# The first block of the input weights asked for by ScalarE's queue, beside x on SyncE's

## The reference, cut to what matters

```python
h = rms_norm(x, attn_norm_w[l])          # x (256, 1024)
proj = h @ w_in[l]                       # w_in (1024, 3072)
dq, dk, dv, lq, lk, lv = jnp.split(proj, split_at, axis=-1)
o_diff = rms_norm(diff_attention(dq, dk, dv, diff_slopes, lam), diff_subln_w[l]) * (1.0 - lam_init)
o_dil = dilated_attention(lq, lk, lv, dil_slopes)
mix = jnp.concatenate([o_diff.reshape(...), o_dil.reshape(...)], axis=-1)
x = x + mix @ w_out[l]
x = x + moe_ffn(rms_norm(x, ffn_norm_w[l]), ...)   # top 4 of 32 experts, 12 MB of weights each
return rms_norm(x, final_norm_w)
```

## Time and profile before

| | us |
|---|---|
| median of 3 runs | 1051.96 (1050.82 to 1052.12) |
| the profiled execution | 1052.54 |
| its span in the trace | 1050.8 |
| PE busy | 1010.7 (96%) |
| VectorE, ScalarE, GpSimd busy | 231.3, 118.1, 21.7 |
| moved by DMA | 423.85 MB, 403 GB/s over the span |

### The profile page before, as it was taken

How to read it: one execution, slowest core, us unless ns; L and a number is a source line. 1 busy time by engine, 2 the same in 40 slices (tenths; PEclk the granted TensorE clock), 3 DMA queues, 4 the chain that set the end, 5 groups by cost and what they waited for, 6 DMA issues and landing times.

```text
span 1050.8 us, 11954 instructions
## 1 busy us (share of the span) xinstructions
PE 1010.7 (96%) x4953; PEld 431.2 (41%) x4953; DVE 231.3 (22%) x515; ACT 118.1 (11%) x275; POOL 21.7 (2%) x39
## 2 busy tenths in 40 slices
PE   9999999999999999999999999898998989899996
PEld 8686543434343434343434333242433333243422
DVE  3766542221111111111111111021211111021111
ACT  1143411110100000000000000000000000000001
POOL 1001400000000000000000000000000000000000
PEclk9999999999999999999999999999999999999999
DMA  9991869999999999999999999999999999999996
GB/s 302 417 408 31 314 240 400 423 427 428 435 430 433 428 430 438 424 435 437 425 435 432 428 437 428 432 438 424 435 434 427 437 430 429 429 426 427 427 424 252
DMA packets 28458, 423.85 MB, mean 403 GB/s; under 512 B 5440, under 2 KB 5456, under 8 KB 11312
## 3 DMA queue, kind: packets, MB, share of 16 engines
q1 hardware_dynamic: 26112, 422.80, 95.3%
q10 hardware_dynamic: 2320, 0.67, 0.3%
HBM read 422.41 MB, written 1.05 MB: 403 GB/s over the span
## 4 chain that ended last, share of the span: by engine, by line
PE 72%; DMA 19%; DVE 5%; another core or an unknown queue 1%; SPq 1%; ACT 1%; issue 1%; DVEq 0%; POOL 0%
PE psum L996 35%; DMA gu_ring<-in_w_gate_up_dram 18%; PE psum L1047 11%; PE psum L1069 5%; PE psum L953 4%; PE psum L663 3%; PE psum L821 3%; PE psum L710 3%; PE psum L686 3%; DVE mixed L1494 2%; DVE mixed L1490 1%; DVE mixed L1492 1%; PE psum L706 1%; PE psum L692 1%
## 5 line engine op out<-in xcount | busy, mean ns | idle before, releaser
L996 PE MATMUL psum<-gu_ring,mixed 128*64 128x512 f32 x2048 | 455.3, 601 | 21.7 <-DMA gu_ring<-in_w_gate_up_dram 21.4
L996 PEld LDWEIGHTS psum<-gu_ring,mixed 128*64 128x64 f32 x2048 | 145.4, 138 | 310.4 <-issue 271.3
L1490 DVE TENSOR_SCALAR mixed<-psum 128x512 f32<-128x512 f32 x32 | 22.1, 691 | 411.3 <-PE psum L996 411.3
L1047 PE MATMUL psum<-dn_ring,mixed 128*64 128x512 f32 x352 | 78.0, 595 | 2.2 <-ACT mixed L595 2.2
L1047 PE MATMUL psum<-mixed 128*64 128x512 f32 x352 | 78.0, 595 | 0.0
L1447 DVE TENSOR_TENSOR mixed<-posm,iota 128x256 f32<-128x256 f32 x47 | 19.9, 424 | 243.4 <-PE psum L663 243.0
L613 ACT ACTIVATE mixed<-psum 128x512 f32<-128x512 f32 x30 | 17.9, 597 | 433.2 <-PE psum L996 433.2
L972 PE MATMUL psum<-mixed 64*128 64x512 f32 x256 | 63.6, 615 | 0.7 <-ACT mixed L599 0.7
L953 PE MATMUL psum<-mixed,xres 128*128 128x128 f32 x480 | 56.2, 275 | 0.0
L953 PEld LDWEIGHTS psum<-mixed,xres 128*128 128x128 f32 x480 | 55.2, 193 | 0.0
L663 PE MATMUL psum<-ident,mixed 128*128 128x128 f32 (+1 forms) x251 | 48.1, 300 | 4.2
(11 more groups left out here) (168 smaller groups left out, 537.1 us busy)
## 6 DMA issues: line engine op xcount, KB each, us to landing
gu_ring<-in_w_gate_up_dram SPq DMA_DIRECT2D x44, 4096.0 KB, 45.4
gu_ring<-in_w_gate_up_dram SPq DMA_DIRECT2D x34, 2048.0 KB, 18.7
dn_ring<-in_w_down_dram SPq DMA_DIRECT2D x11, 4096.0 KB, 43.6
mixed<-in_w_down_dram SPq DMA_DIRECT2D x11, 4096.0 KB, 44.8
dn_ring<-in_w_down_dram SPq DMA_DIRECT2D x9, 2048.0 KB, 19.1
mixed<-in_w_down_dram SPq DMA_DIRECT2D x7, 2048.0 KB, 16.5
gu_ring<-in_w_in_dram SPq DMA_DIRECT2D x11, 1024.0 KB, 16.6
gu_ring<-in_w_gate_up_dram SPq DMA_DIRECT2D x10, 1024.0 KB, 8.7
```

The source lines that it names most:

```text
L996: last = mm(bank[b0 + b][CAP * c:CAP * (c + 1), :], xg[:, k, CAP * half:CAP * (half + 1)], group(w, c), start=False, stop=(k == KT - 1), s ...
L1047: last = mm(bank[4][CAP * c:CAP * (c + 1), :], actT[:, a0:a0 + CAP], dn_whole[half][:, k // 2, w0:w0 + 512], start=False, stop=(k == KT - ...
L1490: chain(V.tensor_scalar(up_t, bank[b0 + 1][:, :], 1.0 - LIMIT, 1.0 + LIMIT, ALU.max, ALU.min))
```

## The change

The load of block k = 0 of the first weight group leaves SyncE's list, where it stood behind the two halves of x, and becomes the first instruction of ScalarE's list, ahead of the two norm rows. Source, destination, size and semaphore stay. On SyncE's list block k = 1 now follows x directly.

```diff
@@ block.sync
                 sp.dma_start(xres[:, a, :], xv[:, a, :]).then_inc(x_in[a], 16)
 
             w_in_v = w_in.rearrange("o (k p) c -> p (o k) c", p=P)
-            for k in range(2):
-                sp.dma_start(gu_ring[:, 0, D * k:D * (k + 1)], w_in_v[:, k, 0:D]).then_inc(w_in_first[k], 16)
+            sp.dma_start(gu_ring[:, 0, D:2 * D], w_in_v[:, 1, 0:D]).then_inc(w_in_first[1], 16)
             for g in range(3):
@@ block.scalar
         def _(act):
+            act.dma_start(gu_ring[:, 0, 0:D], w_in.rearrange("o (k p) c -> p (o k) c", p=P)[:, 0, 0:D])\
+                .then_inc(w_in_first[0], 16)
             act.dma_start(prm_rows[0:8, :], attn_norm_w.rearrange("o (k p) -> (o k) p", p=P)).then_inc(prm_in, 16)
             act.dma_start(prm_rows[8:16, :], ffn_norm_w.rearrange("o (k p) -> (o k) p", p=P)).then_inc(prm_in, 16)
```

## The result

| | before | after |
|---|---|---|
| median of 11 runs, us | 1051.3 (1050.56 to 1053.41) | 1054.74 (1053.3 to 1055.51) |
| ratio | | 1.0030, 95% interval 1.0022 to 1.0037 |
| the profiled execution | 1052.54 | 1053.59 |
| its span | 1050.8 | 1051.9 |

The change makes the kernel slower by 3.4 us, 0.3%. The forecast was 1052.9 and "the same"; the range (1050.7 to 1054.8) holds the median, at its upper edge. The eleven times of after say why to be careful with that: five lie between 1053.3 and 1054.1, six between 1054.7 and 1055.5, and the profiled one is of the lower group.

What follows compares the result with a forecast made beforehand. Start bounded by block k=0's transfer among loads on already busy engines; PE 96% busy overall. Three terms of 0 and +0.9 us gave 1053.4 profiled, forecast 1052.9 since the median lies 0.6 below the profiled run; range 1050.7 to 1054.8.

Steps and rivals of the forecast that it cites:

- The wait is worth 0.7 us: Ahead of the first projection matmul: of PE's 1.2 us idle, an earlier weight block can win only 0.7 us.
- Nothing on SyncE's queue, on ScalarE's work or from the norm rows: Start of the kernel: the removed issue, ScalarE's later work and the norm rows behind the block each cost 0.
- The two queues share, x lands late: Start: weights go ahead of x on some engines, x lands late, projection starts at 8.9 to 9.7: +0.5 to +1.3 us.
- in turns of a microsecond or more: First microseconds of DMA: the two queues alternate in long turns, and which starts is nearly a tie.
- the line: Opening 512 KB loads queued for 16 busy engines; first three places delivered at 4.1, 5.4 and 8.3 us.
- the sum: All terms of the start added: three of 0 and +0.9 us for the order of blocks.
- The clock: Rival: PE's clock rises late after idling ahead of x, slowing the first projection; +2.3 to +3.7 with block order; chance 0.15.
- the order of blocks: Start: block k=0 moves from third in line to beside x's first half, delaying x; +0.9 us taken.
- One for one to the end: Whole kernel: a shift of the first projection matmul passes unchanged to the end, in both directions.
- "Slower": Outcome slower by over 0.2% (2.1 us): chance 0.12, of which 0.10 late clock and 0.02 late norm rows.

Runs made afterwards that it cites:

- with 12 fillers: Changed kernel with 12 filler matmuls ahead of x instead of 7: 1052.20 us, ratio 1.0004; the same edit on the kernel before: 1051.74 us, ratio 1.0001.
- before, 2 fillers: Kernel before the change with 2 filler matmuls ahead of x instead of 7, no DMA changed: 1053.45 us, ratio 1.0014.
- block behind the norm rows: Changed kernel with weight block k=0 issued behind the two norm rows on ScalarE's queue instead of ahead of them: 1055.12 us, ratio 1.0032.
- the block behind the exponential: Changed kernel with weight block k=0 issued on ScalarE's queue behind its small exponential: 1056.66 us, ratio 1.0048.
- the bridge: 30 filler matmuls between the turns of x and the projection, added to the kernel with the block behind the exponential: 1056.90 us, ratio 1.0049.

## Why the prediction was right or wrong

- **The wait is worth 0.7 us.** Not contradicted, and not measured: the wait did go, and no kernel is faster than before.
- **Nothing on SyncE's queue, on ScalarE's work or from the norm rows.** Right: k=1 still lands at 9.0, and PE turns the norm rows at 8.36 without waiting for them. In the kernel with both blocks ahead of the norm rows that cover is gone, and PE does wait, 0.67 us.
- **The two queues share, x lands late.** The direction was right, and the runs with x's second half in the weights' place show that it is the load beside x and not the weights. Two things in it were not. The queues do not go "in turns of a microsecond or more": both move within 0.4 us. And the line was taken to deliver at the same pace as before, its second place at 5.4; with both queues loaded it moved 236 GB/s from 2 to 4 us, not 351. So the size of one step was off: I put x's first half in the second place of the line, 5.4; it landed at 6.4 and 5.7 in the two profiles of the change and 5.7 with x's second half beside it. The second half, put at 6.6 to 8.3, landed at 7.8 and 7.1, early enough not to matter: the start follows from the first half alone (6.36 + 2.2 + 1.3 = 9.9, 5.71 + 2.2 + 1.3 = 9.2). Of the starts of the projection 9.25 lies inside the forecast's 8.9 to 9.7, 9.89 just above. Against the +0.9 of the sum these starts are +0.9 and +1.5. No run has this term by itself: with 12 fillers 1.0 us stays by the medians and 0.4 by the ratio, but there the turns of x are faster too (1.06 against 1.94).
- **The clock.** This is the step that failed. It stood among the rivals with 0.15, at +2.3 to +3.7 together with the order of blocks; the measured +3.4 is inside that. The reason given against it, "PE idles 1.2 us ahead of 8.39 now and the matmuls after it are fast", compared an idle gap behind the rise with one ahead of it. The two are not alike: the gap from 4.5 to 6.5 falls where PE has yet to earn the clock. Ahead of the rise, 1.9 us of idle left the 32 records at 9.81 us (before, 2 fillers); behind it, 1.75 us left them at 7.14 (block behind the norm rows), and only 3.43 us brought the clock down. Of 23 timed executions of the change, 13 are at 1054.7 or above; it should have been the likeliest case.
- **One for one to the end.** Right, over the whole 5 us that the experiments cover.
- **The chances.** "Slower" had 0.12, and slower by over 0.2% is what came. That the range held is in part luck: its upper end was drawn through the late clock, a case held unlikely, and the median lies 0.06 us inside it; the sum by itself had 1052.9. The step from +0.9 to +3.4 is about the clock's 2.6 us, shown from three sides: taken away by fillers in the change (-2.6), brought by fewer fillers in the kernel before (+2.2), and read in the records (634 ns against 379). Between the second profile of the change and that with 12 fillers the front moves by 18.06 - 15.71 = 2.35 us: 0.55 of it by an earlier start, 1.8 by faster records.

## What to carry to other kernels

When a late transfer is asked for earlier, ask which transfer ahead of it was punctual only because it had the engines alone; here a second queue took about half the bytes from it and added none. At the start of a kernel PE's idle gaps can cost twice, by their length and by a clock that rises late: filler matmuls must last until the operand that they wait for really lands, so their number has to be looked at again whenever that landing moves. And times that fall into two groups call for a profile of each group before anything is concluded from one.

## What the runs showed of the hardware that was not expected

- The clock column of the profile says 1.00 from the start of the span, also where the records show the lower level: until 4.3 us, wherever PE works in the traces here, one record of 128 columns comes every 0.21 us, against 0.11 later. Only the fall and the rise behind the first rise are in it (0.50 from 9.8 to 16.6 us in the kernel with the block behind the exponential).
- The same program gets its clock early or late from one execution to the next, and not by the length of the gap alone: in the change the 32 first records of the projection took 7.17 us in one, behind 2.01 us of idle, and 8.98 in another, behind 1.36. With PE at work without a gap from 1.13 us, the 24 records of 12 fillers took 4.38, 5.19 and 5.49 us in three kernels: the pace doubled near 4.4 us, near 6.0, and only in the turns of x behind them.
- With both queues loaded from the start, DMA moved 233 to 297 GB/s from 2 to 4 us, against 336 to 360 on one queue, and yet the third block of 512 KB landed no later: at 7.8, 7.1 and 7.1 us (the change twice, x's second half on ScalarE's queue), and at 8.3, 8.0 and 8.1 where one queue held all (before, with 2 and with 12 fillers). That isn't the single queue as such: in the kernel with the block behind the exponential the third block on SyncE's queue landed at 7.1, with the bridge at 8.0. Why stays open.
